# Expert stage of a diffusion trunk: gathering the second table's rows in turn with the next tile's rows of the first

## The reference, cut to what matters

```python
v1, i1 = lax.top_k(s1, PEER_TOPK)
v2, i2 = lax.top_k(s2, PEER_TOPK)
cand = (v1[..., :, None] + v2[..., None, :]).reshape(PEER_BLOCK, PEER_HEADS, PEER_TOPK * PEER_TOPK)
cand_idx = (i1[..., :, None] * PEER_N_KEYS + i2[..., None, :]).reshape(PEER_BLOCK, PEER_HEADS, PEER_TOPK * PEER_TOPK)
best, pos = lax.top_k(cand, PEER_TOPK)
idx = jnp.take_along_axis(cand_idx, pos, axis=-1)
g = jax.nn.softmax(best, axis=-1).astype(x.dtype)
act = jax.nn.gelu(jnp.einsum('nhkd,nd->nhk', U[idx], x))
return jnp.einsum('nhk,nhkd->nd', g * act, V[idx])
```

## Time and profile before

| | |
|---|---|
| median of 3 runs | 5730.54 us (5727.5 to 5732.07) |
| the profiled execution | 5728.84 us, its span 5727.0 us |
| VectorE busy | 3823.9 us (67%) |
| TensorE busy | 3320.0 us (58%) |
| GpSimd busy | 2693.9 us (47%) |
| gathers | 1,280 in each layer, 1342 MB in all |
| first gather of each layer | at 1150.5 and 4000.6 us |

### The profile page before, as it was taken

How to read it: one execution, slowest core, us unless ns; L and a number is a source line. 1 busy time by engine, 2 the same in 40 slices (tenths; PEclk the granted TensorE clock), 3 DMA queues, 4 the chain that set the end, 5 groups by cost and what they waited for, 6 DMA issues and landing times. The chain is left out here.

```text
span 5727.0 us, 39565 instructions
## 1 busy us (share of the span) xinstructions
PE 3320.0 (58%) x12262; PEld 1768.2 (31%) x12262; DVE 3823.9 (67%) x7523; ACT 639.3 (11%) x1536; POOL 2693.9 (47%) x2772
## 2 busy tenths in 40 slices
PE   7988837893517062351779888388944170624426
PEld 1457715451102020110214677164511020201102
DVE  1136545379797997978410365553897979989784
ACT  0012113111001010000100121131110010101001
POOL 0012210157777777777600122101577777777776
PEclk9989957997859587785989899589978595967859
DMA  6200000199999999999961000002999999999999
GB/s 225 74 8 2 1 7 1 66 338 399 409 403 410 409 399 409 398 409 402 393 216 50 8 2 1 7 1 79 358 405 410 408 409 406 402 408 399 408 403 369
DMA packets 432729, 1476.74 MB, mean 258 GB/s; under 512 B 45828, under 2 KB 50436, under 8 KB 430852
## 3 DMA queue, kind: packets, MB, share of 16 engines
q0 software_dynamic: 368640, 1342.34, 59.2%
q1 hardware_dynamic: 63880, 131.87, 6.5%
HBM read 1462.34 MB, written 11.70 MB: 257 GB/s over the span
## 5 line engine op out<-in xcount | busy, mean ns | idle before, releaser
L1589 PE MATMUL ps<-z,o 128*128 128x512 f32 x2560 | 1256.0, 618 | 708.5 <-ACT o L1502 355.7
L1621 DVE CUSTOM_DVE_ANT_0 z<-z,ps 128x1024 f32<-128x1024 f32 x1280 | 1530.3, 1217 | 65.4 <-DMA z<-in_peer_u,experts 27.3
L1444 POOL DMA_INDIRECT z<-in_peer_u,experts x1280 | 1210.7, 946 | 569.4 <-DVE state L1621 256.2
L1444 POOL DMA_INDIRECT z<-in_peer_v,experts x1280 | 1212.8, 948 | 460.3 <-issue 295.4
L1646 DVE SCALAR_TENSOR_TENSOR ps<-z,state,ps 128x1024 f32<-128x1024 f32 x630 | 808.6, 1283 | 393.7 <-DMA z<-in_peer_v,experts 393.3
L1589 PEld LDWEIGHTS ps<-z,o 128*128 128x128 f32 x2560 | 447.8, 193 | 1511.7 <-ACT o L1502 935.3
L1517 PE MATMUL ps<-const,hT 128*128 128x128 f32 x80 | 17.8, 395 | 1163.2 <-ACT o L1502 1163.2
L1517 PEld LDWEIGHTS ps<-const,hT 128*128 128x128 f32 x80 | 14.4, 206 | 1168.4 <-ACT o L1502 1014.8
L401 PE MATMUL ps<-w,hT 128*128 128x512 f32 (+1 forms) x960 | 365.6, 543 | 1.8 <-DVE hT L371 1.8
L1502 ACT ACTIVATE o<-const,state 128x128 f32<-128x128 f32 x640 | 244.3, 399 | 1069.0 <-PE ps L1589 1064.4
L376 DVE COPY z<-ps 128x512 f32<-128x512 f32 (+1 forms) x30 | 19.3, 642 | 342.8 <-PE ps L401 342.8
(11 more groups left out here) (355 smaller groups left out, 4648.7 us busy)
## 6 DMA issues: line engine op xcount, KB each, us to landing
w<-in_w_mod SPq DMA_DIRECT2D x24, 2048.0 KB, 8.0
w<-in_w_in SPq DMA_DIRECT2D x10, 2048.0 KB, 10.8
z<-in_peer_u,experts POOLq DMA_INDIRECT x1280, 13.4
z<-in_peer_v,experts POOLq DMA_INDIRECT x1280, 12.1
w<-in_peer_wq SPq DMA_DIRECT2D x8, 2048.0 KB, 12.6
w<-in_w_out SPq DMA_DIRECT2D x4, 2048.0 KB, 14.2
scores<-rows SPq DMA_DIRECT2D x8, 1024.0 KB, 9.5
gate<-scores SPq DMA_DIRECT2D x8, 1024.0 KB, 8.0
```

What stands on the lines that cost most here:

```text
L1444: eng.indirect_dma_start(m.ring[j % RING], None, at_layer_rows(table), bass.IndirectOffsetOnAxis(ap=m.experts[:, t % 2, k:k + 1], axis=0)) ...
L1589: mm = eng.matmul(m.ps[:, 4 + n, :], m.diag[:, (done + q) % DIAGS, :], row_j[:, n * 512:(n + 1) * 512], start=(q == 0), stop=(q == SLOTS / ...
L1621: eng.tensor_tensor_reduce(row_j, row_j, h_rows, 1.0, 0.0, ALU.mult, ALU.add, m.acts[:, k:k + 1]).then_inc(used_v, 1)
```

## The change

From the V rows of tile 1 on, the gathers alternate: V row k of tile t, then U row k of tile t+1, for t = 1, 2, 3. The V rows of tile 4 have no partner. Tile 0 and the U rows of tile 1 keep their order. `fetched_rows` writes the order out, and `by_tensor` says who adds a V row up: TensorE takes three of four rows in tile 0, all rows in tiles 1, 2 and 3, and every other one in tile 4. The ranking runs two tiles ahead: tiles 1 and 2 are both ranked among the V rows of tile 0, two steps after each slot below 84, and the ranking of tile t+2 lies among the dot products of tile t+1. For that the experts have three buffers and the softmax shares two.

```diff
+def fetched_rows():
+    order = [(0, table, k) for table in range(2) for k in range(SLOTS)] + [(1, 0, k) for k in range(SLOTS)]
+    for t in range(1, TILES - 1):
+        order += [row for k in range(SLOTS) for row in ((t, 1, k), (t + 1, 0, k))]
+    return order + [(TILES - 1, 1, k) for k in range(SLOTS)]
+
+def by_tensor(row):
+    t, table, k = row
+    return table == 1 and {0: k % 4 != 3, TILES - 1: k % 2 == 0}.get(t, True)
...
-                for t in range(TILES):
-                    if t > 0:
-                        for k in range(SLOTS):
-                            dot(t, k)
-                    weigh(t)
+                weigh(0)
+                for k in range(SLOTS):
+                    if not by_tensor((0, 1, k)):
+                        add_row(0, k, k == 3)
+                    for i in range(2 * k, min(2 * k + 2, 2 * RANK_STEPS)):
+                        rank_step(eng, m, o, sems, 1 + i // RANK_STEPS, i % RANK_STEPS)
+                residual(0)
+                for k in range(SLOTS):
+                    dot(1, k)
+                weigh(1)
+                for t in range(1, TILES - 1):
                     for k in range(SLOTS):
-                        if not by_tensor(k):
-                            add_row(t, k)
-                        if t + 1 < TILES and k < RANK_STEPS:
-                            rank_step(eng, m, o, sems, t + 1, k)
+                        dot(t + 1, k)
+                        if t + 2 < TILES and k < RANK_STEPS:
+                            rank_step(eng, m, o, sems, t + 2, k)
                     residual(t)
+                    weigh(t + 1)
+                for k in range(SLOTS):
+                    if not by_tensor((TILES - 1, 1, k)):
+                        add_row(TILES - 1, k, k == 1)
+                residual(TILES - 1)
...
                 def residual(t):
...
-                    eng.tensor_tensor(m.sum, m.sum, acc, ALU.add).then_inc(sums, 1)
+                    if not all(by_tensor((t, 1, k)) for k in range(SLOTS)):
+                        eng.tensor_tensor(m.sum, m.sum, acc, ALU.add).then_inc(sums, 1)
+                    else:
+                        eng.sem_inc(sums, 1)
```

More of the change, by code:

```diff
@@ L7 @@
+import itertools
 from contextlib import ExitStack, contextmanager
@@ L1296, in rank_step @@
         else:
-            o.mark(eng.tensor_tensor(m.share.rearrange("p (h k) -> p h k", h=HEADS), m.shifted, bc(inverses, 2, TOPK), ALU.mult))
+            o.mark(eng.tensor_tensor(m.share[t % 2].rearrange("p (h k) -> p h k", h=HEADS), m.shifted, bc(inverses, 2, TOPK), ALU.mult))
         return
@@ L1370, in stage_experts @@
     REST = TOK - P
-    JOBS = TILES * 2 * SLOTS
+    ROWS = fetched_rows()
+    AT = {row: j for j, row in enumerate(ROWS)}
+    BY_T = list(itertools.accumulate(by_tensor(row) for row in ROWS))
+    EXP_AFTER = {0: ((1, 44), (2, 88)), **{t: ((t + 2, 84),) for t in range(1, TILES - 2)}}
+    OF_T = [row for row in ROWS if by_tensor(row)]
     XS = m.xs
@@ L1392, in loads_of, with used, row_here @@
         def loads_of(r):
-            return len(range(r, JOBS, RING))
-        def row_here(eng, j):
+            return len(range(r, len(ROWS), RING))
+        def used(row):
+            j = AT[row]
+            return j + 1 - BY_T[j], BY_T[j]
+        def row_here(eng, row):
+            j = AT[row]
             r = j % RING
@@ L1430, in _ @@
                 eng.wait_ge(*rest_turned("chunk", KC - 1))
-                for t in range(TILES):
-                    for phase, table in enumerate((m.inp["peer_u"], m.inp["peer_v"])):
-                        for k in range(SLOTS):
[L1434 to L1446, removed]
+                for j, (t, table, k) in enumerate(ROWS):
+                    if table == 0 and k % (2 * TOPK) == 0:
+                        eng.wait_ge(sems.experts_ready, HEADS // 2 * t + k // (2 * TOPK) + 1)
+                    if j >= RING:
+                        by_v, by_t = used(ROWS[j - RING])
+                        if by_tensor(ROWS[j - RING]):
+                            eng.wait_ge(used_t, by_t)
+                        else:
+                            eng.wait_ge(used_v, by_v)
+                    eng.indirect_dma_start(m.ring[j % RING], None, at_layer_rows(m.inp[("peer_u", "peer_v")[table]]),
+                                           bass.IndirectOffsetOnAxis(ap=m.experts[:, t % 3, k:k + 1], axis=0)).then_inc(
+                        row_loaded[j % RING], 16)
             @block.scalar
@@ L1577, in _ @@
                 eng.wait_ge(*rest_s_kept("list", PER * NB - 1))
[L1578 to L1591, removed]
+                for q, (t, table, k) in enumerate(OF_T):
+                    eng.wait_ge(diags_ready, q + 1)
+                    if k == 0 and t + 1 < TILES:
+                        turn_h(t + 1)
+                    if k == 0 and t > 0:
+                        eng.wait_ge(sum_kept, t)
+                    here = row_here(eng, (t, 1, k))
+                    last = q + 1 == len(OF_T) or OF_T[q + 1][0] != t
+                    for n in range(2):
+                        mm = eng.matmul(m.ps[:, 4 + n, :], m.diag[:, q % DIAGS, :], here[:, n * 512:(n + 1) * 512],
+                                        start=(k == 0), stop=last)
+                    mm.then_inc(used_t, 1)
             @block.vector
@@ L1629, in weigh @@
                     o.after(0)
-                    gelu(eng.scalar_tensor_tensor(m.acts, m.acts, 0.5, m.share, ALU.mult, ALU.mult))
+                    gelu(eng.scalar_tensor_tensor(m.acts, m.acts, 0.5, m.share[t % 2], ALU.mult, ALU.mult))
                     if t > 0:
-                        eng.wait_ge(used_t, t * SLOTS // 2)
+                        eng.wait_ge(used_t, used((t - 1, 1, SLOTS - 1))[1])
                     eng.wait_ge(tanh_ready, t + 1)
```

71 lines of the change are left out of this document (32 added, 39 removed).

## The result

The changed kernel takes 5780.42 us (median of 4 runs, 5778.95 to 5782.46) against 5731.31 us before (4 runs, 5727.5 to 5732.33). The ratio is 1.0088 with a 95% interval of 1.0074 to 1.0102, so it is slower by 49 us. Forecast were 5787 us, in 5765 to 5808. The profiled execution took 5781.61 us, its span is 5779.8 us.

What follows compares the result with a forecast made beforehand. The prediction took DMA transfers, at about 410 GB/s in the expert stages, to bound the kernel. 5728.84 + 61.4 (VectorE's delay in tile 0) - 5.2 (score fetches) = 5785.0, plus 1.7 to the median: 5787 us, range 5765 to 5808.

Steps and rivals of the forecast that it cites:

- What bounds the kernel: Expert stages: transfers set the pace at about 410 GB/s, 1.28 us a row, with some ten gathers queued.
- Term 1: Tile 0's V rows: two rankings and 21 adds take VectorE 149.6 us, delaying row 96; +61.4 us over two layers.
- Term 2: Score fetches of 1 MB, 2.6 us each: tile 3's moves into tile 0's V rows and costs nothing there; -5.2 us.
- Term 3: Alternating V and U rows: VectorE and TensorE both fit in a pair's 2.56 us, so the pace stays; 0.
- Term 4: Turn of a tile: 11.4 us, first V row used 8.9 after landing, ring covers 12.3, so hidden; 0.
- without a hole in the DMA: Sign expected at the turns of a tile: they last 11 to 12 us and the DMA shows no gap.
- B: Rival: after row 96 rows land at GpSimd's 1.24 us, making up the delay; no change, 5729; chance 0.07.
- C: Rival: about 5 us disappear at each of six V stretches with ranking, -30; delay also made up, 5699; chance 0.04.
- D: Rival: residual, weights and layout outlast the ring's cover by 8.9 us at each of six turns; +53, 5840; chance 0.09.
- E: Rival: TensorE's clock falls to 0.5 in the alternating pairs, a row takes 3.44 us; +676, about 6460; chance 0.02.

Runs made afterwards that it cites:

- control: The changed kernel as it is, run once more on chip 13 beside the other kernels: 5782.06 us against 5727.85 before, ratio 1.0091.
- tile 0 kernel: Changed kernel with tiles 1 to 4 in the order of before, VectorE again adding every other V row there: 5786.57 us, 1.01 on chip 13; 1.0097 on chip 0.
- spread kernel: Changed kernel with the 168 ranking steps spread over all 128 slots of tile 0's V rows: 5722.73 us, 0.9991 on chip 13; 1.0006 on chip 0.

## Why the prediction was right, step by step

**What bounds the kernel: right.** Once a stretch is supplied, it runs at 401 to 409 GB/s whatever VectorE and TensorE do: with VectorE at 217 or 294 us of work in 256 rows.

**Term 1, VectorE in tile 0's V rows: right, and the source of the loss.** The ranking and 21 adds took 150.7 us from start to the end of row 83's add, forecast 149.6, with no waits but 0.9 us for the exponentials. Pricing the ranking by the one place where it runs alone was the right choice: by the price that it has among today's adds it would have been 142 us. The gather of row 96 was issued 0.3 us later and took 5.3 us to land, not 4.2:

```profile
z<-in_peer_v,experts POOLq DMA_INDIRECT x1, 5.3
```

So row 96 of tile 0 landed at 4401.2, 374.4 us after the layer's first gather at 4026.8. Before it was 4341.4 after 4000.6, that is 340.8: 33.6 us later, forecast 31.2. The window from first to last issue is 38.9 us longer, and at 202.9 us longer than the 195 forecast; the 5.3 us between 38.9 and 33.6 delay the issues and not the landings: before, row 96 was issued 10.6 us ahead of its landing, now 5.3. Spreading the same steps removes it (5782.06 to 5722.73). Tile 0 alone makes it (1.0100 for 1.0091). And giving VectorE more adds and TensorE fewer rows makes it worse, which excludes TensorE.

**Term 2, score fetches: right.** No run took a fetch away, but the landings show what one costs. In layer 2 of the kernel before, the fetch for tile 3 landed at 4643.8, and V rows 71 and 72 of tile 1 landed 3.4 and 1.6 us after the row ahead of each, 5.05 in place of 2.56: 2.5 us lost, forecast 2.6. Behind row 96 the kernel before has two such fetches in a layer, the changed one has one (landed at 4786.0).

**Term 3, alternating rows: right to 4.5 us.** They keep 2.56 us a pair; here a product of the ranking, the longest step, stands between two dot products with 0.19 us to spare:

```profile
4650.23 1.22 DVE L1629 CUSTOM_DVE_ANT_0 z<-z,ps 128x1024 f32<-128x1024 f32 x1 [0.19 <-DMA z<-in_peer_u,experts]
4651.38 0.08 DVE L1629 DVE_READ_ACCUMULATOR2_ANT state<- 128x1 f32 x1
4651.38 1.22 DVE L1336 TENSOR_TENSOR o<-o 128x1024 f32<-128x1024 f32 x1
4652.79 1.22 DVE L1629 CUSTOM_DVE_ANT_0 z<-z,ps 128x1024 f32<-128x1024 f32 x1 [0.19 <-DMA z<-in_peer_u,experts]
```

Against U and V rows one after the other they are 4.5 us better over two layers (control against the tile 0 kernel, medians of 4 runs each, whose ranges are 7 and 6 us wide and don't overlap). Forecast was 0. The prediction's price for gathers that take GpSimd longer beside ranking products, 8 us a tile, was too high: over all 2,560 gathers of the kernel before the mean is 0.95 us, so the 1.98 of the earlier trace rows is rare.

**Term 4, the turns: hidden, as forecast, but with nothing to spare.** From the last V row of tile 1 to the first use of tile 2's V rows all went as counted: TensorE begins that row at 4938.49 and the next tile's first at 4947.93, 9.4 us apart, forecast 9.5. Windows of 5 us over this turn of the changed kernel, layer 2:

```profile
4945.00:4950.00 5.00, 3.83 (x11) 2.78 (x12) 2.26 (x7) 2.70 (x9) 0.00 (x0) 0.50 1.04 411
4950.00:4955.00 5.00, 5.00 (x11) 2.05 (x10) 5.00 (x23) 0.82 (x3) 2.61 (x3) 0.87 0.62 205
4955.00:4960.00 5.00, 5.00 (x13) 2.16 (x12) 5.00 (x20) 1.18 (x3) 3.78 (x5) 1.00 0.93 313
4960.00:4965.00 5.00, 5.00 (x13) 2.20 (x12) 5.00 (x13) 1.21 (x3) 3.78 (x5) 1.00 0.97 379
4965.00:4970.00 5.00, 3.92 (x10) 1.29 (x9) 3.97 (x12) 1.20 (x3) 3.78 (x5) 1.00 1.03 419
```

The first V row itself took longer than counted. TensorE had stood idle for 5.7 us, from 4940.4 to 4946.2, and its granted clock is 0.50 from 4946 to 4949.5, the level of 1.2 GHz. The row was done only when ScalarE made its next diagonal:

```profile
4951.55 0.40 ACT L1511 ACTIVATE o<-const,state 128x128 f32<-128x128 f32 x1 [3.38 <-PE ps L1598]
4951.78 0.94 POOL L1454 DMA_INDIRECT z<-in_peer_u,experts  x1 [8.11 <-PE ps L1598]
```

That is 3.6 us after its start, forecast 1.9. The row had landed at 4940.9 (issued at 4926.61, 14.3 us to landing), so its buffer came free 10.6 us later, forecast 8.9. The gather that waited for it took 5.6 us to land, forecast 4.3:

```profile
z<-in_peer_u,experts POOLq DMA_INDIRECT x1, 5.6
```

It landed at 4957.4, 16.5 us after the row whose buffer it took, and 13 rows at 1.28 are 16.6. So the 3.4 us of spare cover were in truth 0.1. The next rows slipped a little: those issued at 4954.27, 4955.51 and 4956.75 took 5.8, 6.3 and 6.7 us and landed 1.5 to 1.7 us after the row ahead of each. Together this turn cost about 0.7 us, the third double turn about 0.3, the first nothing. In layer 1, and in both layers of the second trace of this kernel, no row slipped at a turn.

The windows seem to say more: the missing share is (205 + 97 + 31) x 5 / 410 = 4 us of transfer, so the forecast "without a hole in the DMA" was wrong. But this is not lost time. From 4950 to 4955 four rows landed (4951.2, 4952.4, 4953.6 and 4954.8), which are 2.1 MB, and only 1.0 MB was moved: the rest had been moved before 4950. What the hole uses up is the queue, from 14 us between issue and landing to 5.6. The kernel before has such holes as well, for instance here after tile 1's V rows, where its rows went on landing 1.24 to 1.29 us apart:

```profile
4722.00:4727.00 5.00, 0.00 (x0) 0.00 (x0) 5.00 (x9) 0.00 (x0) 3.11 (x4) 0.50 0.99 371
4727.00:4732.00 5.00, 0.00 (x0) 0.00 (x0) 5.00 (x11) 0.00 (x0) 3.78 (x5) 0.50 0.93 338
```

So the turns did not stand bare with 13 buffers. With 9 the same 16.5 us meet 9 x 1.28 = 11.5, an estimate of 5.0 us a double turn, near the 4.9 above; on chip 13, where landings can be read, 9 buffers were not run.

**The sum.** Against the profiled execution it was +56.2 and is +52.8. Two errors partly cancel, so that the total came this close is in part luck. Row 96 comes 33.6 and 32.8 us later in the two layers, 2.4 and 2.6 more than forecast; in layer 2 the ranking has 1.1 of that and the restart 1.1. From row 96 to its last landing layer 2 took 1363.4 us against 1370.4 before, and layer 1 took 1364.5 against 1371.0. So 7.0 and 6.5 us came back, where 2.6 were forecast.

What came back beyond the fetch stands in single rows. Apart from those at a fetch, 36 rows behind row 96 in the two layers of the kernel before land more than 2 us after the row ahead, most of them 2.2, where 1.28 is the rule. The tile 0 kernel has 29 of them, the two traces of the changed kernel 21 and 23. At 0.9 us each 15 fewer are an estimated 14 us, more than enough for the 8.3 that were not forecast. In the kernel before each of the 18 in layer 2 has a fetch of 8 KB on an instruction queue (q14 in the trace) 1.5 to 3 us ahead of its landing, but not every such fetch has a late row. Why the changed kernel has fewer, and whether the fetches are the cause, no run tests.

**The rivals.** B (landing at GpSimd's pace after the delay) is excluded: after the delay the U rows of tile 1 were issued in 159.6 us, 1.25 us each, but they landed 1.28 us apart at 409 GB/s as ever, so the queue only grew again. By the port ceiling of 435 GB/s, which the Trainium skill gives in "DMA: Bandwidth & Descriptors", "Where 436 GB/s comes from", a row would take an estimated 1.20 us, and the rows could have caught up at GpSimd's pace. The trace disagrees: no window of 128 rows or more goes over 409, and 419 in one window of 5 us is the most shown here. C came in a small way only: 4.5 us for the alternating rows, where 30 were its price. D needed a turn longer than the cover, by 8.9 us; in layer 2 it took 10.9 us from landing to the next issue, against a cover of 16.6 - 5.6 = 11.0, and cost 0.7 us. E did not come: within the alternating rows the clock fell at the turns only, for the first row.

## What to carry to other kernels

Where a stage is bound by transfers through a ring, the average load of an engine doesn't tell whether it holds the ring: look at the time it needs for each buffer, slot by slot, against the pace at which buffers arrive. 168 small steps packed at two a slot cost 1%, and the same steps at 1.31 a slot cost nothing that can be measured, though the engine's total is the same. And price work that is going to stand alone by a place where it stands alone: among other instructions dependent steps hide their gaps, and the price of a head pair comes out 8% too low (14.4 for 15.6 us). The same holds for a ring's cover: a hole in the bytes moved is not yet a late row, so look at when the rows land.

The change as made loses 0.9%; with its ranking spread it is level with the kernel before (0.9991, 0.9981 to 1.0001), since what it frees on VectorE was never on the path.

## What the runs showed that was not expected

Chips 0 and 2 moved about 370 GB/s in the same stages, 10% less, for the same kernels: 6042 to 6044 us against 5728 to 5731. The rows are not evenly slower there. In the spread kernel on chip 0 many dot products of the alternating rows stand 2.55 to 2.57 us apart, as on chip 13, and others 3 to 8.5. In the traces of chip 0 small dependent VectorE operations, those of the weights, also stood some 0.4 us apart at the start of tile 0's V rows, where chip 13 has 0.03 to 0.1. Why is not known. The tile 0 kernel is slower there as here; the ratio of the spread kernel is 1.0006 there and 0.9991 on chip 13, and the intervals overlap.
